# Two-layer hybrid decoder trunk: four units of the conditioning product moved behind the feed-forward's start on GpSimd, and channel sums added on VectorE before one product of ones

## The reference

```python
mod = silu(c) @ ada_w[l] + ada_b[l]                # 6 x 1024 values
sh1, sc1, g1, sh2, sc2, g2 = split(mod, 6)
h = rmsnorm(x, norm1_w[l]) * (1 + sc1) + sh1
mix = token_mixer(h)                               # below
x = x + g1 * mix
h = rmsnorm(x, norm2_w[l]) * (1 + sc2) + sh2
f = swiglu(h) if l == 0 else moe(h)                # moe: top 2 of 8 experts
x = x + g2 * f
```

## Time and profile before

| | |
|---|---|
| runs | 1905.03 us median of 3 (1898.22 to 1906.97) |
| the profiled execution | 1905.59 us, of which the span in the trace is 1903.8 us |
| TensorE busy | 1785.8 us (94%) |
| VectorE, ScalarE, GpSimd busy | 475.8 us (25%), 282.6 us (15%), 354.3 us (19%) |
| granted TensorE clock | 0.977 of full speed, mean over the span |
| the chain that ended last | PE 83%, DMA 8%, issue 3%, ACT 2%, DVE 2% |

### The profile page before, as it was taken

How to read it: one execution, slowest core, us unless ns; L and a number is a source line. 1 busy time by engine, 2 the same in 40 slices (tenths; PEclk the granted TensorE clock), 3 DMA queues, 4 the chain that set the end, 5 groups by cost and what they waited for, 6 DMA issues and landing times.

```text
span 1903.8 us, 28350 instructions
## 1 busy us (share of the span) xinstructions
PE 1785.8 (94%) x11341; PEld 1307.7 (69%) x11342; DVE 475.8 (25%) x1044; ACT 282.6 (15%) x572; POOL 354.3 (19%) x215
## 2 busy tenths in 40 slices
PE   7999999999999999999989998979998998999896
PEld 5888878878888788888866866566554443444442
DVE  1694455110000295322323001101100100101101
ACT  2204333010000211434021000000000100000001
POOL 2707192069998000000000000000000000000000
PEclk8999999999999999999999999989999999999999
DMA  9745475167665444345466979899998999999994
GB/s 400 255 153 197 150 259 182 56 254 281 255 246 211 162 155 142 124 144 166 177 242 265 418 289 417 329 418 361 417 419 345 388 421 417 418 418 418 414 421 181
DMA packets 86831, 541.92 MB, mean 285 GB/s; under 512 B 8752, under 2 KB 21072, under 8 KB 21840
## 3 DMA queue, kind: packets, MB, share of 16 engines
q1 hardware_dynamic: 67824, 490.24, 65.2%
q0 software_dynamic: 5760, 41.95, 5.9%
q10 hardware_dynamic: 13024, 6.82, 1.3%
HBM read 537.89 MB, written 1.08 MB: 283 GB/s over the span
## 4 chain that ended last, share of the span: by engine, by line
PE 83%; DMA 8%; issue 3%; ACT 2%; DVE 2%; SPq 1%; ACTq 0%; DVEq 0%
PE ps L779 21%; PE ps L1220 12%; PE ps L854 8%; PE ps L871 8%; PE ps L1368 6%; PE ps L1259 6%; PE ps L878 4%; PE ps L1298 3%; PE ps L1389 3%; DMA ring<-in_moe_units 2%; DMA sq<-in_moe_units 2%; PE ps L1330 2%; DMA aring<-in_moe_units 2%; DMA misc<-in_moe_units 1%; DMA misc<-in_ada_units 1%
## 5 line engine op out<-in xcount | busy, mean ns | idle before, releaser
L779 PE MATMUL ps<-hT,ring 128*128 128x256 f32 x1984 | 438.5, 382 | 1.0 <-ACT hT L1495 1.0
L779 PEld LDWEIGHTS ps<-hT,ring 128*128 128x128 f32 x1984 | 377.1, 191 | 56.2 <-issue 5.1
L696 POOL TENSOR_TENSOR aring<-aring,ccol 128x2048 f32<-128x2048 f32 x40 | 144.6, 3614 | 212.1 <-ACT hT L1495 97.6
L702 POOL TENSOR_TENSOR aring<-aring 128x1024 f32<-128x1024 f32 x80 | 152.1, 1901 | 6.3
L871 PE MATMUL ps<-hT,ring 128*128 128x256 f32 x672 | 146.7, 379 | 0.0
L1220 PE MATMUL ps<-ring,hT 128*64 128x256 f32 (+2 forms) x1152 | 131.7, 364 | 7.9 <-issue 5.7
L871 PEld LDWEIGHTS ps<-hT,ring 128*128 128x128 f32 x672 | 127.0, 190 | 16.9
L1220 PEld LDWEIGHTS ps<-ring,hT 128*64 128x64 f32 (+2 forms) x1152 | 75.0, 133 | 59.7 <-issue 37.9
L1892 DVE SCALAR_TENSOR_TENSOR misc<-cpad,par,misc 128x256 f32<-128x256 f32 x240 | 102.7, 509 | 0.0
L2218 DVE TENSOR_TENSOR proj<-proj,ps 128x256 f32<-128x256 f32 (+2 forms) x28 | 14.6, 521 | 350.9 <-PE ps L1220 350.9
L1500 ACT ACTIVATE proj<-ps 128x512 f32<-128x512 f32 x64 | 38.2, 597 | 313.9 <-PE ps L779 301.1
(11 more groups left out here) (381 smaller groups left out, 1975.5 us busy)
## 6 DMA issues: line engine op xcount, KB each, us to landing
ring<-in_moe_units SPq DMA_DIRECT2D x144, 1024.0 KB, 19.2
ring<-in_dense_units SPq DMA_DIRECT2D x121, 1024.0 KB, 5.0
aring<-in_moe_units SPq DMA_DIRECT2D x48, 1024.0 KB, 18.6
proj<-in_moe_units SPq DMA_DIRECT2D x48, 1024.0 KB, 20.0
aring<-in_ada_units POOLq DMA_DIRECT2D x40, 1024.0 KB, 6.8
extra<-in_moe_units SPq DMA_DIRECT2D x24, 1024.0 KB, 18.6
scan<-in_moe_units SPq DMA_DIRECT2D x24, 1024.0 KB, 20.7
misc<-in_moe_units SPq DMA_DIRECT2D x24, 1024.0 KB, 21.1
```

Source lines behind the costliest of these rows:

```text
L696: last = g.tensor_tensor(w, w, ccol[:, :].unsqueeze(2).broadcast_to([P, KT, 256]), ALU.mult)
L702: last = g.tensor_tensor(dst, w[:, 0:half_k, :], w[:, half_k:2 * half_k, :], ALU.add)
L779: last = mm(ps[:, n % 2, j * SEQ:(j + 1) * SEQ], wide(s)[:, k, j * P:(j + 1) * P], hT[:, k, :], start=(k == 0), stop=(k == KT - 1))
```

## The change

It has two parts. The first: GpSimd's wait for the feed-forward's input stands before unit 20 of layer 0 and no longer before unit 24, so units 20 to 23 are done behind it, ahead of layer 1's 24. Their two pairs are transposed and reduced in the feed-forward: of the 14 pairs, `TURN_AT` says how many have been turned by the end of each group (0, 1, 2, 3, 4, 5, 6, 8, 10, 11, 12), and two stand behind the loop, ahead of the last down product as before. The pairs of layer 0 use the banks of layer 1's, the bias of the late columns (`modc` 40 to 47, used by L2014) is added behind the last reduction, and the pairs' old places in the mixer (after `y_batch` 6, and after the first state-space pair) go away.

The second: VectorE adds four tiles to one before each sum over 512 channels, so that one product of ones is left of four. For the mean the additions stand behind the convolution and ahead of the short ones, and the product moves behind chunk 16; for the variance they stand behind L1917; for the groups they stand behind the merge of the second convolution pair, the product moves from behind the third to behind the fourth pair of `out_pair`, and on VectorE the merge of the first attention pair moves ahead of the reciprocal. Two semaphores change their names and use; one increment by ScalarE that nobody waited for goes.

```diff
@@ -43,6 +43,10 @@
 ADA_SLOTS = 2
 ADA_EARLY = 13
 ADA_PAUSE = 17
+ADA_LATE = 20
+LATE = ADA_LATE // 2
+ADA_TURNS = [(0, q) for q in range(LATE, ADA_CHUNKS // 2)] + [(1, q) for q in range(ADA_CHUNKS // 2)]
+TURN_AT = (0, 1, 2, 3, 4, 5, 6, 8, 10, 11, 12)
 ADA_BANK = (3, 6)
 HALF, QUARTER = 64, 32
 SIZES = (QUARTER, HALF, 96, 128, 160, 256)
@@ -255,7 +259,7 @@
             return proj[:, GATE + 4 + a, :] if a < 20 else sq[:, a - 16, :]
 
         def ada_bank(l, q):
-            return 7 if l == 0 and 2 * q >= ADA_FIRST else ADA_BANK[l] + q % 2
+            return 7 if l == 0 and ADA_FIRST <= 2 * q < ADA_LATE else ADA_BANK[1] + q % 2
 
         slot_i = sc[:, 0, 0:SEQ].bitcast(i32)
         rt = cdec[:, :, :].rearrange("p a b -> p (a b)")[:, 0:20 * TT * EXPERTS].rearrange(
@@ -687,7 +691,7 @@
                 a, slot = n % ADA_CHUNKS, (n + 1) % ADA_SLOTS
                 if n == ADA_EARLY:
                     pool.wait_ge(xv_s, 3)
-                if n == ADA_CHUNKS:
+                if n == ADA_LATE:
                     pool.wait_ge(h_s, 2 * KT)
                 if n == ADA_PAUSE:
                     pool.wait_ge(ao_s, 4)
@@ -761,9 +765,9 @@
 
                 n = (ADA_CHUNKS * l + 2 * q - ADA_FIRST) // 2
                 pe.wait_ge(apool_s, 2 * n + 2)
-                if l == 0 and n:
+                if l == 0 and 0 < q < LATE and n:
                     pe.wait_ge(ared_s, n)
-                elif l:
+                elif l or q >= LATE:
                     pe.wait_ge(ared_s, n - 1)
                 for j in range(4):
                     last = nc.tensor.transpose(ps[:, ada_bank(l, q), j * P:(j + 1) * P],
@@ -924,11 +928,9 @@
                 for n in range(2 + LOOPED, 16):
                     w_next(n)
 
-                pe.wait_ge(cv_s, CV0 + (l + 1) * CT * CONF_TAPS)
-                for k in range(CT):
-                    last = mm(ps[:, 2, 0:SEQ], ones[:, :], cacc[:, k, :], start=(k == 0), stop=(k == CT - 1))
-                last.then_inc(cm_s, 1)
                 w_next(16)
+                pe.wait_ge(csum_s, 2 * l + 1)
+                mm(ps[:, 2, 0:SEQ], ones[:, :], csq[:, 2, :], start=True, stop=True).then_inc(cm_s, 1)
                 w_next(17)
                 w_next(18)
 
@@ -953,11 +955,9 @@
                 last.then_inc(ac_s, 1)
                 w_next(19)
 
-                pe.wait_ge(csq_s, l + 1)
+                pe.wait_ge(csum_s, 2 * l + 2)
                 pe.wait_ge(acs_s, l + 1)
-                for k in range(CT):
-                    last = mm(ps[:, 2, 0:SEQ], ones[:, :], csq[:, k, :], start=(k == 0), stop=(k == CT - 1))
-                last.then_inc(cvar_s, 1)
+                mm(ps[:, 2, 0:SEQ], ones[:, :], csq[:, 2, :], start=True, stop=True).then_inc(cvar_s, 1)
 
                 for i in range(12):
                     w_next(20 + i)
@@ -1002,7 +1002,8 @@
                         if l == 0:
                             if i == 5:
                                 pe.wait_ge(ao_s, 4)
-                            ada_transpose(0, i - 1)
+                            if i - 1 < LATE:
+                                ada_transpose(0, i - 1)
 
                 pe.wait_ge(cu_s, l + 1)
                 for idx in range(4):
@@ -1013,14 +1014,12 @@
                     out_pair(l, idx, s, half, CT, 2 * (idx % 2), cacc)
                     if idx == 0:
                         y_batch(l, 7)
-                    if idx == 2:
-                        pe.wait_ge(gsq_s, 2 * (l + 1))
+                    if idx == 3:
+                        pe.wait_ge(gsum_s, l + 1)
                         if l == 0:
-                            pe.wait_ge(ared_s, (ADA_CHUNKS - ADA_FIRST) // 2 - 1)
+                            pe.wait_ge(ared_s, (ADA_LATE - ADA_FIRST) // 2)
                         for g in range(GROUPS):
-                            for k in range(4):
-                                last = mm(ps[:, 7, g * SEQ:(g + 1) * SEQ], ones[:, :], ysq[:, 4 * g + k, :],
-                                          start=(k == 0), stop=(k == 3))
+                            last = mm(ps[:, 7, g * SEQ:(g + 1) * SEQ], ones[:, :], ysq[:, 4 * g + 2, :], start=True, stop=True)
                         last.then_inc(gst_s, 1)
                 for idx in range(4):
                     s, n = slot_of(("attn", l, idx // 2))
@@ -1031,8 +1030,6 @@
                     s, n = slot_of(("ssm", l, idx))
                     pe.wait_ge(full[s], n)
                     out_pair(l, 8 + idx, s, wide, KT, 0, proj[:, Z:Z + 8, :])
-                    if l == 0 and idx == 0:
-                        ada_transpose(0, ADA_CHUNKS // 2 - 1)
                 for idx in range(4):
                     s, n = slot_of(("mix", l, idx))
                     pe.wait_ge(full[s], n)
@@ -1058,9 +1055,10 @@
                             down(dsl, (g - 1) % 2, g == 1, False)
 
                         if g:
-                            ada_transpose(1, g - 1)
-                    for q in range(GD - 1, ADA_CHUNKS // 2):
-                        ada_transpose(1, q)
+                            for n in range(TURN_AT[g - 1], TURN_AT[g]):
+                                ada_transpose(*ADA_TURNS[n])
+                    for turned in ADA_TURNS[TURN_AT[GD - 1]:]:
+                        ada_transpose(*turned)
                     dsl, dn = slot_of(("d", 0, GD - 1))
                     pe.wait_ge(full[dsl], dn)
                     pe.wait_ge(hm_s, HM0 + 2 * GD)
@@ -1891,6 +1889,9 @@
                         dve.wait_ge(cv_s, k * CT + C0 + m + 1 - CT)
                         v.scalar_tensor_tensor(cacc[:, m, :], cpad[:, m, ds(k, SEQ)], cwcol[:, l, ds(k * CT + m, 1)],
                                                cacc[:, m, :], ALU.mult, ALU.add).then_inc(cv_s, 1)
+                dve.wait_ge(cv_s, CV0 + (l + 1) * CT * CONF_TAPS)
+                then_wait(v.tensor_tensor(csq[:, 0:2, :], cacc[:, 0:2, :], cacc[:, 2:4, :], ALU.add))
+                v.tensor_tensor(csq[:, 2, :], csq[:, 0, :], csq[:, 1, :], ALU.add).then_inc(csum_s, 1)
                 for q in range(3):
                     dve.wait_ge(ev_s, 2 + W_CHUNKS * l + XBC // 2 + 2 * q + 2)
                     for tap in range(SSM_TAPS - 1, -1, -1):
@@ -1915,6 +1916,9 @@
                 v.tensor_copy(acum_t[:, :], ps[0:HEADS_S, 2, 0:SEQ])
                 then_wait(v.tensor_copy(acum[:, :, :], ps[:, 2, 336:368].rearrange("p (a b) -> p a b", a=2)))
                 v.tensor_tensor(dec[:, 0, :], ps[:, 2, 368:384], acum[:, 0, :], ALU.subtract).then_inc(acs_s, 1)
+                dve.wait_ge(csq_s, l + 1)
+                then_wait(v.tensor_tensor(csq[:, 0:2, :], csq[:, 0:2, :], csq[:, 2:4, :], ALU.add))
+                v.tensor_tensor(csq[:, 2, :], csq[:, 0, :], csq[:, 1, :], ALU.add).then_inc(csum_s, 1)
                 dve.wait_ge(cvar_s, l + 1)
                 v.tensor_scalar(rs[:, 0, :], ps[:, 2, 0:SEQ], 1.0 / CONF_WIDTH, EPS, ALU.mult, ALU.add).then_inc(cvr_s, 1)
                 dve.wait_ge(csd_s, l + 1)
@@ -1948,7 +1952,7 @@
                     v.tensor_copy(ao[:, i - 1, :], ps[:, 7, (i - 1) % 2 * SEQ:(i - 1) % 2 * SEQ + SEQ]).then_inc(ao_s, 1)
                 for k in range(8):
                     lmat(l, k)
-                    if l == 0 and k:
+                    if l == 0 and k and 3 + k < LATE:
                         ada_reduce(0, 3 + k, modc)
                     if k >= 2 and k % 2 == 0:
                         y_out(l, k // 2 - 1)
@@ -1969,15 +1973,20 @@
                     v.tensor_tensor(merged[:, 2 * idx:2 * idx + 2, :], merged[:, 2 * idx:2 * idx + 2, :], g,
                                     ALU.add).then_inc(mg_s, 1)
 
-                for idx in range(3):
+                for idx in range(2):
+                    merge_conf(idx)
+                dve.wait_ge(gsq_s, 2 * (l + 1))
+                groups = ysq.rearrange("p (g a) n -> p g a n", g=GROUPS)
+                then_wait(v.tensor_tensor(groups[:, :, 0:2, :], groups[:, :, 0:2, :], groups[:, :, 2:4, :], ALU.add))
+                v.tensor_tensor(groups[:, :, 2, :], groups[:, :, 0, :], groups[:, :, 1, :], ALU.add).then_inc(gsum_s, 1)
+                for idx in range(2, 4):
                     merge_conf(idx)
                 dve.wait_ge(gst_s, l + 1)
                 v.tensor_scalar(gr[:, 0, :, :], ps[:, 7, :].rearrange("p (a b) -> p a b", a=2), 1.0 / 512, EPS,
                                 ALU.mult, ALU.add).then_inc(gv_s, 1)
-                merge_conf(3)
+                merge_add(4, 0, GATE + 16)
                 dve.wait_ge(gsd_s, l + 1)
                 then_wait(v.reciprocal(gr[:, 2, :, :], gr[:, 1, :, :]))
-                merge_add(4, 0, GATE + 16)
                 for m in range(KT):
                     last = v.scalar_tensor_tensor(proj[:, Z + m, :], proj[:, Z + m, :], pcol[:, l, R_SN + m:R_SN + m + 1],
                                                   gr[:, 2, m // 4, :], ALU.mult, ALU.mult)
@@ -1987,8 +1996,7 @@
                 for idx in range(4):
```

(17 more changed lines are left out.)

## The result

| | before | changed |
|---|---|---|
| median (lowest to highest) | 1904.07 (1898.22 to 1906.97), 4 runs | 1929.85 (1926.57 to 1932.01), 4 runs |
| ratio to before | | 1.0149, 95% interval 1.0127 to 1.0171 |
| profiled execution / its span | 1905.59 / 1903.8 | 1932.01 / 1930.2 |
| TensorE, VectorE, GpSimd busy | 1785.8, 475.8, 354.3 | 1779.7, 474.0, 352.2 |

What follows compares the result with a forecast made beforehand. TensorE, busy 94% of the span, was taken as the bound, with GpSimd full during the feed-forward. Terms +29.0 + 2.1 - 5.25 - 0.44 - 0.2 - 2.6 + 2.8 = +25.4 us on 1905.6 gave 1931, range 1918 to 1939.

Steps and rivals of the forecast that it cites:

- Units, feed-forward side: End of feed-forward: last down product waits for GpSimd's 28 units, +29.0 us, plus +2.1 for lower clock and slower transposes.
- Units, mixer side: Layer 0's state-space chunks from 28 on: without GpSimd's units VectorE's products no longer delay TensorE, -5.25 us.
- Transposes: Layer 0's mixer: removed transposes behind `y_batch` 6 give nothing, those behind the first state-space pair -0.44 us.
- Mean and variance, layer 0: Fewer products save 2.6 us on TensorE, but VectorE and GpSimd sharing leaves -0.2; bounds -2.6 and +1.2.
- Group sums: Both layers: 2.6 us saved is lost waiting before the fourth attention pair; lower clock adds +1.4 per layer.
- Layer 1: Mean and variance sums in layer 1: GpSimd is done and VectorE idles, so -2.6 us; bounds -2.6 and -1.3.
- The sums keep their gain: Rival: VectorE's chain has unseen slack and no clock loss, another -10.4 us in all, 1920.6; chance 0.17.
- The wait costs more: Rival: 3.1 us clock ramp, late loads, the variance's bounds add +6 to +8 us, 1938; chance 0.13.
- The moved units are hidden: Rival: at 8.0 us per unit or less the last down product doesn't wait; 1900 or 1889.5; chance 0.04.
- The change doesn't do what it says: Rival: pairs behind the loop weren't needed before the last down product, or mixer contention came from elsewhere; about 1914; chance 0.05.

Runs made afterwards that it cites:

- The two-unit run: Changed kernel with only units 22 and 23 moved behind the feed-forward's input instead of four: 1914.90 us, ratio 1.0066 to the kernel before.
- the run with the other four units moved on: Changed kernel with the reciprocal before the first attention merge and layer 1's last four units waiting for layer 1's first norm: 1892.17 us, ratio 0.9948.
- the sums alone: Changed kernel with GpSimd's units, their transposes and reductions as before, leaving only the additions and single products: 1900.04 us, ratio 0.9995.
- with the reciprocal first: Kernel before plus the changed additions and single products, with the reciprocal ahead of the first attention merge: 1893.37 us, ratio 0.9955.
- with unit 16 gone: Changed kernel with GpSimd's wait for the attention ahead of unit 16 instead of 17: 1928.39 us in one run.
- the last kernel: Changed kernel, reciprocal before the first attention merge, layer 1's last four units behind its first norm, GpSimd's attention wait before unit 16: 1890.19 us, ratio 0.9945.
- The run with the reciprocal first: Changed kernel with the group norm's reciprocal back ahead of the first attention merge on VectorE: 1921.88 us, ratio 1.0102.
- the second execution of the changed kernel: Changed kernel unaltered, measured again beside the last experiments: 1927.97 us, ratio 1.0146 to the kernel before.
- the run without the pause: Kernel before without GpSimd's wait ahead of unit 17, so units 17 to 23 follow unit 16 at once: 1912.93 us, ratio 1.0053.

## Why the prediction was right, point by point

**Units, feed-forward side: right.** 253.7 us to the last unit's end were forecast, 254.5 came; +29.0 +2.1 became +32.3. The rest is 0.4 us more for the lower clock (2.5 for the transposes and the product, 2.1 forecast) and a load that landed late:

```profile
429.77 3.59 POOL L700 TENSOR_TENSOR aring<-aring,ccol 128x2048 f32<-128x2048 f32 x1 [1.80 <-DMA aring<-in_ada_units]
```

The forecast had such loads at nothing beyond the 0.63 us that the profile before holds. Ten of the twelve profiles have one of 0.2 to 1.8 us, with units moved or not; why it lands late was not looked into. The pairs inside the loop cost nothing that shows, as said: one waited 0.74 us for GpSimd, which sets the end anyway. The two-unit run settles that it is GpSimd's pace that counts, and the run with the other four units moved on that the feed-forward has no second bound near.

**Units, mixer side: right for the profile that it was read from, whose phase was the costliest of the three seen with these units there.** 5.96 against 5.25. The 8.85 us that I took for an undisturbed step to the next chunk held a wait of 0.21 us for VectorE; undisturbed it is 264.95 - 256.38 = 8.57. That is 0.28 twice, and some 0.2 lie ahead of these chunks. But the gain is against one profiled execution. Other executions of the old order waited 3.18 us at one later place (the sums alone) or 1.75 (with the reciprocal first), and from the state products to the group sums they took 80.1 and 77.1 us where the changed kernel takes 76.5: 3.6 and 0.6 us lost. A term taken from one profile had no range, and should have had: 0 to 6.

**Transposes: right.** Those behind `y_batch` 6 gave nothing: the third pair now waits 1.52 us instead of 1.18, and from the last chunk to it both kernels take 17.60.

**Mean and variance, layer 0: mechanism right, size off.** -0.2 was forecast, -1.76 came, and by phase the runs gave between 0 (the sums alone) and -1.76. The step that failed is the time at which the score operations begin. From the changed kernel's timeline:

```profile
174.84 2.15 DVE L1920 TENSOR_TENSOR cpad<-cpad 128x512 f32<-128x512 f32 x1
177.03 2.45 DVE L1921 TENSOR_TENSOR cpad<-cpad 128x256 f32<-128x256 f32 x1
...
182.32 3.61 POOL L700 TENSOR_TENSOR aring<-aring,ccol 128x2048 f32<-128x2048 f32 x1
...
194.72 0.54 DVE L1815 SCALAR_TENSOR_TENSOR heads<-ps,amask 128x384 f32<-128x384 f32 x1
...
199.28 0.55 PE L820 MATMUL ps<-ident,heads 128*128 128x128 f32 x3 [0.54 <-DVE heads L1827]
```

This execution was 1.55 us later at chunk 16. With that taken out, unit 16 starts at 182.32 - 1.55 = 180.8 and not at 181.6, and the first score operation at 194.72 - 1.55 = 193.2 and not at 194.5: 1.3 of the 1.6 us missed. The rest is that TensorE turns head 0 first and head 1 second, where the forecast had it wait for both; head 0 was there in time, and it waited 0.54 us for head 1. The seven runs with these sums and unit 16 in its old place all have those 0.54 or 0.55 us, and five of them 0.48 to 1.37 more ahead of head 0, so that the forecast's phase does occur. The lock-step of the two engines was right: additions of 0.69 and 0.42 us took 2.15 and 2.45 here, and with unit 16 gone TensorE got its 2.6 us. By the rule cited of the Trainium skill, page "SBUF — State Buffer", section "Who interferes with whom", one waits out the other's whole instruction: the trace of the last kernel agrees, with 3.92 us for a 0.69 us product that came 0.25 us behind a multiplication of 3.62.

**Group sums: right.** 2.6 us of wait forecast, 2.58 measured, in both layers. The +1.4 for the clock was low by 0.3, by the same wrong step as above: against two undisturbed steps (8.08 + 8.57 us) the 21.16 us held 1.7 beyond the wait of 2.84, which is what came. The run with the reciprocal first shows the cause by taking it away.

**Layer 1: right.** To its third pair -2.4 us came, for -2.6.

**Rivals.** "The sums keep their gain" would have needed the tail at 74.44 - 2.58 - 1.7 = 70.2; it was 74.4. "The wait costs more" was near: it had the late loads and the clock. "The moved units are hidden" needed 8.0 us per unit; it was 9.1 still. "The change doesn't do what it says" fell with GpSimd named as the releaser of both transposes. The seven stretches of the table missed by 0.5 to 1.6 us each and in both directions, and add up to 1.0: that 1931 came within 1.2 us of the median was partly luck.

## What to carry to other kernels

An engine that is busy a fifth of the time can be full in one stage: count its work between the event that frees it and the instruction that waits for it, and move work there only up to the difference (6 us here, against 36 moved). What may go further is what nobody needs soon; look for that first. And when products are taken off a path, follow the consumer's chain to the next wait: one merge placed ahead of the reciprocal decided whether the sums were worth 9.9 us or 0.9, by the medians.

## What the runs showed that was not expected

The same wait of 2.57 or 2.58 us ahead of the fourth attention pair was followed by the lower level of TensorE's clock (1.2 of 2.4 GHz) in eight of its ten occurrences and not in the other two (one of them in the second execution of the changed kernel). The tail took 74.3 to 74.4 us with it and 72.7 or 72.8 without, a cost of 1.7 us. At the `y_batch` products a wait of 2.84 us was followed by it in the kernel before, and so was one of 3.18 us in the sums alone (granted clock 0.73 over the 6.3 us behind); one of 2.84 us with two units moved was not (1.00 over the 6.4 us behind), nor was one of 2.81 us in the last kernel, while one of 2.52 us in the run without the pause was (0.73 over 6.3 us). The two windows behind the same wait of 2.58 us, from the second execution of the changed kernel and from the first:

```profile
319.05:325.35 6.30, 6.30 (x29) 5.56 (x30) 2.50 (x4) 0.00 (x0) 0.00 (x0) 1.00 0.26 72
320.20:326.50 6.30, 6.30 (x22) 5.26 (x23) 2.00 (x4) 0.00 (x0) 0.00 (x0) 0.73 0.00 0
```

And what the sharing between VectorE and GpSimd costs swings between executions of kernels with the same instructions there, by a phase of a few tenths of a microsecond: by up to 1.8 us from chunk 16 to the state products, and by some 5 from there to the output pairs. It is one part of the spread of the runs. The other two, 3.5 us ahead of chunk 16 and 6 us in the routing and the experts, stand in stretches that the change does not touch, and their cause was not tested.
